# RG-LRU without reciprocals, its block-diagonal gates between the dense halves, their weights outside the ring

## What is computed

```python
xc = conv4(xa) + conv_b                                   # causal, per feature
gates = einsum("bsnc,knce->kbsne", xb, w_gates) + b_gates  # 8 blocks of 128x128, k = 0, 1
r, i = sigmoid(gates[0]), sigmoid(gates[1])
log_a = -8 * r * softplus(-lam)
a = exp(log_a)
u = sqrt(-expm1(2 * log_a)) * (i * xc)
h[t] = a[t] * h[t-1] + u[t]                               # associative scan
y_a = h * gelu(ga)
```

## Time and profile before

| | |
|---|---|
| median of 3 runs | 2349.78 us (2349.71 to 2351.39) |
| the profiled execution | 2353.49 us |
| its span, first to last instruction | 2351.7 us |
| mean granted TensorE clock | 0.984 |
| PE / DVE / ACT / POOL busy | 2281.4 / 1474.1 / 919.0 / 248.5 us |
| waits of TensorE up to 340 us | 22 us in 9 places |

### The profile page before, as it was taken

One profiled execution on the slowest core, in us unless ns is written; L12 is line 12 of the kernel. 1 busy time (PEld: TensorE's weight loads), 2 busy tenths in 40 slices (PEclk: granted clock), 3 DMA queues, 4 the chain that ended last, 5 costly groups with the idle time before them and its releaser, 6 DMA issues.

```text
span 2351.7 us, 33475 instructions
## 1 busy us (share of the span) xinstructions
PE 2281.4 (97%) x14276; PEld 1983.6 (84%) x14276; DVE 1474.1 (63%) x1936; ACT 919.0 (39%) x1331; POOL 248.5 (11%) x238
## 2 busy tenths in 40 slices
PE   8899998999999999999999999999999999998999
PEld 7899885789998888888859888888888888978998
DVE  6585548577768776756877776335754433976554
ACT  6653435454454222124454212223322222545443
POOL 0030000201111101010020101000100101201110
PEclk9999998899999999999999999999999999999999
DMA  6544370356654454433202544223454322622543
GB/s 239 188 178 163 128 261 33 125 198 233 238 192 167 161 210 187 171 126 113 108 1 108 215 170 188 108 76 114 187 197 162 143 99 84 177 72 93 195 180 108
DMA packets 35393, 358.24 MB, mean 152 GB/s; under 512 B 4029, under 2 KB 6269, under 8 KB 9004
## 3 DMA queue, kind: packets, MB, share of 16 engines
q1 hardware_dynamic: 31788, 343.54, 38.9%
q0 software_dynamic: 3456, 12.56, 1.9%
HBM read 353.11 MB, written 1.13 MB: 151 GB/s over the span
## 4 chain that ended last, share of the span: by engine, by line
PE 88%; DVE 7%; ACT 3%; issue 1%; DMA 1%; POOLq 0%; SPq 0%; DVEq 0%; ACTq 0%
PE psum L861 25%; PE psum L860 25%; PE psum L862 25%; PE psum L924 2%; PE psum L923 2%; PE psum L925 2%; PE psum L1200 1%; PE psum L1226 1%; DVE ring_r L1938 1%; PE psum L1271 1%; DVE rr L1948 1%; DVE small L2465 1%; DVE zT L1967 1%; PE psum L1155 1%; DVE zT_r L1978 0%
## 5 line engine op out<-in xcount | busy, mean ns | idle before, releaser
L860 PE MATMUL psum<-arena_r 128*128 128x256 f32 (+1 forms) x3144 | 1058.8, 337 | 10.4 <-DVE ring_r L1938 4.3
L862 PE MATMUL psum<-arena_r,ring_r 128*128 128x256 f32 (+1 forms) x3144 | 1052.7, 335 | 0.0
L861 PE MATMUL psum<-zT_r,arena_r 128*128 128x256 f32 (+1 forms) x2592 | 848.4, 327 | 0.0
L1440 ACT ACTIVATE arena_r<-ring 128x2048 fp32r<-128x2048 f32 (+1 forms) x252 | 473.3, 1880 | 700.3 <-PE psum L862 651.2
L1938 DVE TENSOR_TENSOR ring_r<-ring,arena_r 128x2048 fp32r<-128x2048 f32 (+1 forms) x252 | 569.5, 2261 | 215.4 <-ACT arena_r L1440 214.5
L860 PEld LDWEIGHTS psum<-arena_r 128*128 128x128 f32 x3144 | 592.2, 188 | 85.7 <-issue 13.1
L862 PEld LDWEIGHTS psum<-arena_r,ring_r 128*128 128x128 f32 x3144 | 595.1, 189 | 65.3
L861 PEld LDWEIGHTS psum<-zT_r,arena_r 128*128 128x128 f32 x2592 | 489.6, 189 | 43.9
L861 PE MATMUL psum<-arena_r 128*128 128x256 f32 (+1 forms) x1128 | 373.4, 331 | 0.0
L2091 DVE CUSTOM_DVE_ANT_0 psum<-arena,cb 128x1024 f32<-128x1024 f32 x256 | 318.0, 1301 | 0.0
L861 PEld LDWEIGHTS psum<-arena_r 128*128 128x128 f32 x1128 | 212.4, 188 | 22.1
(11 more groups left out here) (316 smaller groups left out, 2234.3 us busy)
## 6 DMA issues: line engine op xcount, KB each, us to landing
ring<-in_wf SPq DMA_DIRECT2D x75, 2048.0 KB, 7.6
ring<-in_w SPq DMA_DIRECT2D x41, 2048.0 KB, 7.7
arena<-in_w SPq DMA_DIRECT2D x72, 1024.0 KB, 9.5
ring<-in_wf SPq DMA_DIRECT2D x10, 1536.0 KB, 6.5
ring<-in_w SPq DMA_DIRECT2D x5, 1024.0 KB, 5.3
arena<-strip_scratch POOLq DMA_DIRECT2D x1, 2048.0 KB, 9.5
arena<-rpb_scratch POOLq DMA_DIRECT2D x16, 128.0 KB, 11.3
xT<-in_x SPq DMA_DIRECT2D x1, 1024.0 KB, 5.7
```

Source lines behind the costliest of these rows:

```text
L860: mm(b[c][:, at], whc, xh[:, k, at], start=(k == ks[0]), stop=False)
L861: mm(b[c][:, at], whc, xl[:, k, at], start=False, stop=False)
L862: last = mm(b[c][:, at], wlc, xh[:, k, at], start=False, stop=(k == ks[-1]))
L1440: A(W_hi[h % NHI][:, 0:n], ring[:, half_slot(h)], ACT.Identity).then_inc(sig("w_hi"), 1)
```

## The change

The plan puts the gates in two groups of eight tiles: `lru_gates0` (blocks 0 to 3) behind `lru_g1`, and `lru_gates1` (blocks 4 to 7) behind `small`; `lru_g2` and `lru_g3` come after. The gates' weights are no chunk of the ring any more: SyncE sends them once to `A_w`, an area that `C_q` and `C_k` use later, behind the rest of the constants. Each group of sigmoids stands directly behind the work before it on ScalarE; `w_hi` of the next halves stands behind the group.

The reciprocals go: with 1 - a^2 = t (1 + a^2), VectorE squares a and makes (a^2 + 1) t in one scalar_tensor_tensor, and ScalarE takes the root without a scale. For this exp is done before the `gla_q` copies, and the root before the `gla_k` copies. VectorE's calls of `w_lo` and its other work are put in a new order, with scans ahead of the copies of `gla_v0`.

```diff
--- before.py
+++ after.py
@@ -216,9 +216,11 @@
     add("strip", None, "V")
     add("norm0", None, "A")
     split_pairs("lru_x", 2, W8_LRU_X, "AA")
-    split_pairs("lru_g", 2, W8_LRU_G, "AA")
+    split("lru_g0", "lru_g1", w8(W8_LRU_G), "AA")
+    add("lru_gates0", None, "A" * KT)
     one_half("small", ("w4", 2, HALF), "A")
-    add("lru_gates", ("w4", 0, 2048), "A" * 16)
+    add("lru_gates1", None, "A" * KT)
+    split("lru_g2", "lru_g3", w8(W8_LRU_G + 1), "AA")
     split_pairs("gla_q", 1, W8_GQK, "AA")
     split_pairs("gla_k", 1, W8_GQK + 1, "AA")
     add("gla_al", None, "AAAA")
@@ -477,6 +479,7 @@
         A_yl = part(6144, KT, S)
         A_xc = area(8216, KT, S)
         A_g = area(10264, KT, S)
+        A_w = area(16408, 2048)
         A_r = area(12312, KT, S)
         A_yh = part(12312, KT, S)
         A_i = area(14360, KT, S)
@@ -666,6 +669,7 @@
                     continue
                 if i == NSLOT:
                     sp.dma_start(cst[:, CST_FIRST:CST_OH], d["cst"][:, CST_FIRST:CST_OH]).then_inc(sig("cst_rest_in"), 16)
+                    sp.dma_start(A_w, d["w4"][0, :, 0:2048]).then_inc(sig("lru_gates_in"), 16)
                 if i >= NSLOT:
 
                     _, name, count = CHUNKS[i - NSLOT]
@@ -990,9 +994,18 @@
             for c in range(4):
                 split_features(HALF_AT[f"lru_x{c}"], S, h_hi, z_lo, before=split_ready(0, 0) if c == 0 else None,
                                both=c == 0)
-            for c in range(4):
+            def lru_gates(i):
+                w = A_w.rearrange("p (g n e) -> p g n e", g=2, n=8)
+                pe.wait_ge(sig("lru_gates_in"), 16)
+                for k in range(4 * i, 4 * i + 4):
+                    pe.wait_ge(sig("lru_xc"), k + 1)
+                    for g in range(2):
+                        b = open_tile(TILE[f"lru_gates{i}"] + 2 * (k % 4) + g)
+                        mm(b[:, 0:S], w[:, g, k, :], A_xc[:, k, :], start=True, stop=True).then_inc(filled, 1)
+
+            for c in range(2):
                 split_features(HALF_AT[f"lru_g{c}"], S, h_hi, z_lo)
-
+            lru_gates(0)
             h = HALF_AT["small"]
             wh, wl, _ = half_weights(h)
             b = open_tile(TILE["small"])
@@ -1002,13 +1015,9 @@
                 last = mm(b[:, 0:S], wl[:, k, 0:P], h_hi[:, k, :], start=False, stop=(k == KT - 1))
             last.then_inc(filled, 1)
 
-            w = get("lru_gates").rearrange("p (g n e) -> p g n e", g=2, n=8)
-            for k in range(KT):
-                pe.wait_ge(sig("lru_xc"), k + 1)
-                for g in range(2):
-                    n = TILE["lru_gates"] + 2 * k + g
-                    b = open_tile(n)
-                    mm(b[:, 0:S], w[:, g, k, :], A_xc[:, k, :], start=True, stop=True).then_inc(filled, 1)
+            lru_gates(1)
+            for c in range(2, 4):
+                split_features(HALF_AT[f"lru_g{c}"], S, h_hi, z_lo)
 
             for name in ("gla_q", "gla_k"):
                 for c in range(2):
@@ -1632,32 +1641,38 @@
             def lru_g(c):
                 copy_tiles(f"lru_g{c}", 2, lambda j: A_g[:, 2 * c + j, :], func=ACT.Gelu_apprx_tanh)
 
-            evac_pairs("lru_g", 3, lru_g)
-            lru_g(3)
+            def lru_gates(i):
+                for k in range(4 * i, 4 * i + 4):
+                    for g, dst in enumerate((A_r, A_i)):
+                        b = empty(TILE[f"lru_gates{i}"] + 2 * (k % 4) + g)
+                        A(dst[:, k, :], b[:, 0:S], ACT.Sigmoid, bias=V("b_gates", 8 * g + k, 1)).then_inc(evac["A"], 1)
+
+            evac_pairs("lru_g", 2, lru_g)
+            act.wait_ge(sig("strip_out"), 16)
+            lru_gates(0)
+            w_hi(HALF_AT["small"] + 2)
             b = empty(TILE["small"])
             A(C_lr, b[64:80, 0:S], ACT.Identity)
             A(C_gate, b[0:48, 0:S], ACT.Sigmoid).then_inc(evac["A"], 1)
-            w_hi(HALF_AT["gla_q0"])
-            w_hi(HALF_AT["gla_q1"])
-            act.wait_ge(sig("strip_out"), 16)
-            for k in range(KT):
-                for g, dst in enumerate((A_r, A_i)):
-                    n = TILE["lru_gates"] + 2 * k + g
-                    b = empty(n)
-                    A(dst[:, k, :], b[:, 0:S], ACT.Sigmoid, bias=V("b_gates", 8 * g + k, 1)).then_inc(evac["A"], 1)
+            lru_gates(1)
+            w_hi(HALF_AT["lru_g2"] + 2)
+            lru_g(2)
             act.wait_ge(sig("lru_coef"), 1)
-            wait_evac(act, TILE["lru_gates"] + 15)
+            wait_evac(act, TILE["lru_gates1"] + 7)
             for k in range(KT):
                 A(A_t[:, k, :], A_r[:, k, :], ACT.Tanh, scale=small[:, 40 + k:41 + k]).then_inc(sig("lru_tanh"), 1)
+            w_hi(HALF_AT["lru_g3"] + 2)
+            lru_g(3)
+            act.wait_ge(sig("lru_tanh"), KT)
+            for k in range(KT):
+                A(A_r[:, k, :], A_r[:, k, :], ACT.Exp, scale=small[:, 32 + k:33 + k]).then_inc(sig("lru_a"), 1)
 
             def gla_q(c):
                 copy_tiles(f"gla_q{c}", 2, lambda j: C_q[:, 2 * c + j, :], scale=float(P) ** -0.5)
-                if c == 0:
-                    act.wait_ge(sig("lru_tanh"), KT)
-                    for k in range(KT):
-                        A(A_r[:, k, :], A_r[:, k, :], ACT.Exp, scale=small[:, 32 + k:33 + k]).then_inc(sig("lru_a"), 1)
 
             evac_pairs("gla_q", 2, gla_q)
+            act.wait_ge(sig("lru_v"), 1)
+            A(A_t, A_t, ACT.Sqrt).then_inc(sig("lru_root"), 1)
             evac_pairs("gla_k", 2, lambda c: copy_tiles(f"gla_k{c}", 2, lambda j: C_k[:, 2 * c + j, :]))
             for h in range(4):
                 b = empty(TILE["gla_al"] + h)
@@ -1671,8 +1686,6 @@
             A(C_e, C_e, ACT.Ln, bias=C("one")).then_inc(sig("gla_ln"), 1)
             w_hi(HALF_AT["gla_v0"] + 2)
 
-            act.wait_ge(sig("lru_v"), 1)
-            A(A_t, A_t, ACT.Sqrt, scale=2.0).then_inc(sig("lru_root"), 1)
             evac_pairs("gla_v", 4, lambda c: None)
 
             def gla_og(c):
@@ -2265,35 +2278,22 @@
                 .then_inc(sig("lru_coef"), 1)
             dve.wait_ge(sig("cst_rest_in"), 16)
             lo("lru_g1")
+            lo("small")
+            wait_evac(dve, TILE["lru_gates1"] + 7)
+            dve.wait_ge(sig("lru_xc"), KT)
+            link(v.tensor_tensor(out=A_i, in0=A_i, in1=A_xc, op=ALU.mult))
             lo("lru_g2")
             lo("lru_g3")
-            lo("small")
-
-            wait_evac(dve, TILE["lru_gates"] + 15)
-            dve.wait_ge(sig("lru_xc"), KT)
-            link(v.tensor_tensor(out=A_i, in0=A_i, in1=A_xc, op=ALU.mult))
             lo("gla_q0")
-            dve.wait_ge(sig("lru_tanh"), KT)
-
-
-            link(v.tensor_scalar(out=A_xc, in0=A_t, scalar1=1.0, scalar2=None, op0=ALU.add))
-
-            def reciprocals(k0, k1):
-                for k in range(k0, k1):
-                    last = v.reciprocal(A_xc[:, k, :], A_xc[:, k, :])
-                link(last)
-
-            reciprocals(0, 3)
+            dve.wait_ge(sig("lru_a"), KT)
+            link(v.tensor_tensor(out=A_xc, in0=A_r, in1=A_r, op=ALU.mult))
+            v.scalar_tensor_tensor(out=A_t, in0=A_xc, scalar=1.0, in1=A_t, op0=ALU.add, op1=ALU.mult)\
+                .then_inc(sig("lru_v"), 1)
             lo("gla_q1")
-            reciprocals(3, 6)
             lo("gla_k0")
-            reciprocals(6, KT)
+            dve.wait_ge(sig("lru_root"), 1)
+            link(v.tensor_tensor(out=A_i, in0=A_i, in1=A_t, op=ALU.mult))
             lo("gla_k1")
-            v.tensor_tensor(out=A_t, in0=A_t, in1=A_xc, op=ALU.mult).then_inc(sig("lru_v"), 1)
-            lo("gla_v0")
-            dve.wait_ge(sig("lru_root"), 1)
-            dve.wait_ge(sig("lru_a"), KT)
-            link(v.tensor_tensor(out=A_i, in0=A_i, in1=A_t, op=ALU.mult))
 
             def gla_v(c):
                 for t in range(2):
@@ -2311,8 +2311,9 @@
                     v.tensor_tensor(out=A_y[:, k, :], in0=A_xc[:, k, :], in1=A_g[:, k, :], op=ALU.mult)\
                         .then_inc(sig("lru_y"), 1)
 
+            lru_scan(0, 4)
+            lo("gla_v0")
             gla_v(0)
-            lru_scan(0, 4)
             lo("gla_v1")
             gla_v(1)
             lru_y(0, 4)
```

## The result

The changed kernel takes 2335.95 us (median of 4 runs, 2334.02 to 2338.42) against 2349.74 us: the two medians differ by 13.8 us. The ratio on record for these runs is 0.9935, 95% interval 0.9923 to 0.9947, which is 15.3 us (12.5 to 18.1). 10.5 us were forecast, and the median lies just under the lower end of the range (2336.0). The profiled execution is at 2335.51 us with a span of 2333.7, that of before at 2353.49 and 2351.7, so the two traces differ by 18.0 us. So the change is worth 12 to 15 us, single executions of one kernel scatter by several us, and how much of the difference lies in the changed stage has to be read from the traces.

The account below looks back on a forecast made before the run. TensorE, busy 97% of the span, bounds the kernel. Of at most 12.7 us, 0.6, 0.8 and 1.0 are lost, leaving 10.3; the schedule's 10.5 us gives 2349.78 − 10.5 = 2339.3 us, range 2336.0 to 2344.5.

Parts of the forecast that it names:

- The gates: Gate matmuls: waits of 6.2 and 0.8 us and the slow clock go; 0.6 us of waiting comes in.
- The ring: Load of `lru_g2/3`, sent when `lru_x3` ends, lands at 51.8 and costs nothing; gates' 1 MB off the ring priced at nothing.
- Table loads: ScalarE ahead of `gla_k0`: five loads, before two; TensorE waits 0.8 us at `gla_k0`, 1.0 at `gla_k1`.
- rival (a): Tanh sits in the gelu set, all waits but 0.6 us go: 12.1 to 12.4 us gained, 2337.5 us; 27%.
- scalar_tensor_tensor: VectorE's operation on 128x2048: lower bound 2.29 us, upper 3.9, taken as 2.4.
- The clock: Slow clock at the gates is 1.9 of 8.9 us; with 3.8 ahead of L923, at most 12.7 us returns.
- The sum: Whole change: 12.7 − 0.6 − 0.8 − 1.0 = 10.3 us; the schedule's own difference is 10.5 us.
- `gla_v`: Waits of 1.3 and 2.5 us ahead of `gla_v2` and `gla_og0` go; `gla_og0` starts at 127.5 instead of 138.01.
- The margins: At `gla_v`, the two waits of TensorE are covered by 0.7 and 0.3 us.
- (b): ScalarE or VectorE later than counted: gain 3.6 us (2346) by slower table switches, 9 by scalar_tensor_tensor's upper bound; 17%.
- (c): The `lru_g2/3` load lands late, ahead of `lru_g1`'s copies: slower, 2354.4 us if landing takes 22.7 us; 2%.
- (d): Nothing moves by more than 4.7 us, the time being lost again behind 138 us: 2348 us; 4%.

Follow-up runs that it names:

- the second series: The changed kernel, unaltered, timed again against the kernel before: ratio 0.9948 (0.9934 to 0.9962), which is 12.2 us; medians 12.7 us apart.

## Why the prediction was right or wrong

**The gates.** Right in what the schedule does: the wait went with the move, and 0.7 us stayed behind the sigmoid table, for 0.6. "So the stall is an order of the queue" is half of the cause. With the order alone put right, the stall only moved, 4.78 us ahead of `gla_q0`; the other half is that `gla_q`'s weights come late, and the move puts `lru_g2` and `lru_g3` in front of them.

**The ring.** Right, and needed: `lru_g2/3` was late by 1.32 us on ScalarE and cost nothing, and in the ring the same load costs 9.1 us and more. The gates' 1 MB took 25.8 us to land, in time for its use, as counted.

**Table loads.** This step failed. "That is five table loads here, where before there were two" was a choice between two cases that no row could tell apart; there were three (sigmoid, gelu, exp). With it "0.8 us late" at `gla_k0` and "1.0 us" at `gla_k1` fell away, as the prediction's rival (a) had it (27%). The experiment with the two loads put back gave 0.85 and 0.81 us: the schedule was right, the input was not. (By the prediction's own times the first wait is 0.6: the split ends at 89.7, `gla_q1` at 89.1. That is also why its terms sum to 10.3 and its schedule to 10.5.) The Trainium skill, "ScalarE: Activation LUTs", section "Table sets: the hidden batching unit", lists tanh with exp and with sigmoid and calls the set of gelu_apprx_tanh a separate one without saying what it holds; this trace adds that tanh is in it. By the figure of 2.66 us for a switch in the same page's section "What ACT_TABLE_LOAD costs" of the Trainium skill, Ln would, as an estimate, have started 1.3 us later than it did. The trace again has no such drain: Exp ends at 106.28, and Ln starts at 107.60.

**scalar_tensor_tensor.** It took 2.29 us on 128x2048, as a product of two tensors does, the lower bound; 2.4 was taken.

**The clock.** This term was too small, and the bound made from it was wrong. "The slow clock 1.9" was read from one trace, and 12.7 us called the most that the change can return. Against that trace the stage gave 12.5 us, 10.1 of waits and so 2.4 of clock; against the other two traces of the kernel before it gave 15, with the same waits. The bound was one of one execution.

**The sum.** 10.3 by its terms, and 12.5 in the stage by the first pair of traces: 1.8 more by the table loads, 0.5 more by the clock, 0.1 less in the first gates. By the runs it is 13.8 and 12.7 us between the medians, 15.3 and 12.2 by the ratios. Rival (a)'s 12.1 to 12.4 us lies within the interval of the second series (8.9 to 15.5 us) and just outside that of the first (12.5 to 18.1). With the table loads alone put right the forecast is 12.3 us and 2337.5; what the measured median lies below that can be the slow clock and the scatter between executions, and these runs do not part the two: the changed kernel's own reach from 2334.0 to 2345.8 us.

**The rest.** `gla_v`: both waits gone, the split of `gla_v2` at 110.66 with TensorE not stopping. The margins, as far as the rows show them, are about 0.8 and 0.6 us, for 0.7 and 0.3. Behind 160 us nothing differs by more than the kernel before differs from itself; rivals (b), (c) and (d) did not occur.

## What to carry to other kernels

On an engine that works through a list in order, ask of each instruction what it waits for and who stands behind it: putting the sixteen gate tiles between weights that were already there took 7.0 us of waiting down to 0.7, while moving only the late rounded copies behind the evacuations gained nothing. A load that is asked for earlier must also be sent earlier; here the slot it needed was freed by taking a chunk that fits elsewhere out of the ring. And a wait of TensorE costs more than its length when the clock falls behind it, by an amount that differs between executions: take a second trace of the old kernel before calling a number the most that can be gained.

## What the runs showed of the hardware

- Gelu (tanh form) and tanh share a table set: gelu at 71.99 and tanh at 72.27 us have no load between them. A load takes 1.28 us with no time lost behind it: at 106.30, right behind Exp's end, and Ln at 107.60.
- Short waits go with a halved clock in some traces and not in others. With 0.85 and 0.81 us of waiting at 88 and 95 us the granted clock was 0.50 from 104 to 107, and with 0.46 us at 94 it was about 0.7 from 101 to 107; with 0.85 us at 103.8 it stayed at 1.00. The same wait of 2.5 us ahead of `gla_og0` was followed by 0.59 in one trace of the kernel before and by 1.00 in another. The changed kernel had none of these waits and 1.00, in two traces.
- With the same instructions, the stage from merge A to the first feed-forward layer, in which the granted clock was 0.94 to 0.96, took 348.4 to 355.1 us in three executions of one kernel.
- An activation on 128x256 with both scale and bias by pointer took 0.50 us of ScalarE's time in a row of eight (4.04), with a pointer for the scale alone 0.41 (3.30).
